# A decoder trunk on one core: parts of GpSimd's S5 preparation on VectorE and ScalarE, the first layer's gated blocks 0 to 7 moved in pairs, tables spread over more units

## The reference, cut to what matters

```
for layer in range(2):
    if layer == 1: kb, vb, kmean = shared_kv(h, kv_norm, w_kv)
    h = h + 0.5 * swiglu(rmsnorm(h, ffn1_norm[layer]), ffn1_w_in[layer], ffn1_w_out[layer])
    hn = rmsnorm(h, mix_norm[layer])
    h = h + (s5_mixer(hn, ...) if layer == 0 else moba_attention(hn, ...))
    h = h + 0.5 * swiglu(rmsnorm(h, ffn2_norm[layer]), ffn2_w_in[layer], ffn2_w_out[layer])
return rmsnorm(h, final_norm)

swiglu(x) = (silu(g) * u) @ w_out,  g, u = split(x @ w_in)
s5_mixer: lambda = exp(a * dt) (complex, 64 states in 64 groups); B' = f(lambda, a) * b
          x[t] = lambda * x[t-1] + B' u[t];  y = Re(C x) + d * u;  gelu(y) @ w_glu, gated
```

## Time and profile before

| | |
|---|---|
| median of 3 runs | 952.15 us (951.94 to 952.48) |
| the profiled execution | 952.85 us |
| its span, first to last instruction | 951.1 us |
| TensorE busy | 938.9 us, 99% |
| VectorE busy | 622.0 us, 65% |
| ScalarE busy | 502.6 us, 53% |
| GpSimd busy | 184.3 us, 19% |
| DMA | 180.11 MB, 189 GB/s |
| granted TensorE clock | 0.999 |

### The profile page before, as it was taken

How to read it: one execution, slowest core, us unless ns; L and a number is a source line. 1 busy time by engine, 2 the same in 40 slices (tenths; PEclk the granted TensorE clock), 3 DMA queues, 4 the chain that set the end, 5 groups by cost and what they waited for, 6 DMA issues and landing times.

```text
span 951.1 us, 14886 instructions
## 1 busy us (share of the span) xinstructions
PE 938.9 (99%) x5809; PEld 777.5 (82%) x5809; DVE 622.0 (65%) x783; ACT 502.6 (53%) x713; POOL 184.3 (19%) x235
## 2 busy tenths in 40 slices
PE   8999999999999999999999999999999999999997
PEld 7888888888888888888888888888888888888885
DVE  5667977889765666655665666666567565666554
ACT  7654544577555455544654454554458554554441
POOL 2799999901000000000000000000060000000000
PEclk9999999999999999999999999999999999999999
DMA  9856555520355777777678677777751367777761
GB/s 333 292 176 201 181 177 194 177 70 4 115 192 189 216 209 215 214 216 221 219 184 253 174 227 213 220 210 235 220 177 46 112 198 218 211 215 205 188 215 45
DMA packets 137877, 180.11 MB, mean 189 GB/s; under 512 B 95184, under 2 KB 95952, under 8 KB 137808
## 3 DMA queue, kind: packets, MB, share of 16 engines
q1 hardware_dynamic: 137232, 178.33, 61.8%
q10 hardware_dynamic: 576, 0.84, 0.3%
HBM read 167.33 MB, written 1.05 MB: 177 GB/s over the span
## 4 chain that ended last, share of the span: by engine, by line
PE 77%; POOL 16%; issue 2%; ACT 1%; DVE 1%; DMA 1%; SPq 1%; POOLq 0%; ACTq 0%; DVEq 0%
PE ps L1417 75%; POOL tmp L592 7%; POOL sm L592 4%; POOL cp L592 2%; POOL w L592 2%; DMA raw<-in_in 1%; PE ps L1446 1%; POOL rotc L592 0%; POOL skip_eye L720 0%; PE ps L1565 0%; POOL rots L592 0%; POOL w_bd L710 0%; PE ps L1422 0%; SPq L530 0%; ACT pr L1014 0%
## 5 line engine op out<-in xcount | busy, mean ns | idle before, releaser
L1064 DVE TENSOR_TENSOR w_lo<-raw,w_hi 128x1024 fp32r<-128x1024 f32 x309 | 397.4, 1291 | 262.1 <-ACT w_hi L779 260.2
L779 ACT ACTIVATE w_hi<-raw 128x1024 fp32r<-128x1024 f32 x309 | 326.4, 1059 | 317.4 <-PE ps L1417 314.9
L1417 PE MATMUL ps<-w_hi,x_hi 128*128 128x512 f32 x896 | 351.1, 392 | 0.6 <-DVE w_lo L1064 0.6
L1417 PE MATMUL ps<-w_hi,x_lo 128*128 128x512 f32 x896 | 348.8, 389 | 0.0
L1417 PE MATMUL ps<-w_lo,x_hi 128*128 128x512 f32 x896 | 348.7, 389 | 0.0
L1417 PEld LDWEIGHTS ps<-w_hi,x_hi 128*128 128x128 f32 x896 | 168.3, 188 | 37.2 <-DVE w_lo L1064 1.4
L1417 PEld LDWEIGHTS ps<-w_hi,x_lo 128*128 128x128 f32 x896 | 168.2, 188 | 35.5
L1417 PEld LDWEIGHTS ps<-w_lo,x_hi 128*128 128x128 f32 x896 | 168.4, 188 | 33.9
L1417 PE MATMUL ps<-w_hi,hid_hi 128*128 128x512 f32 x352 | 137.2, 390 | 0.0
L1417 PE MATMUL ps<-w_hi,hid_lo 128*128 128x512 f32 x352 | 136.9, 389 | 0.0
L1417 PE MATMUL ps<-w_lo,hid_hi 128*128 128x512 f32 x352 | 136.9, 389 | 0.0
(11 more groups left out here) (163 smaller groups left out, 612.5 us busy)
## 6 DMA issues: line engine op xcount, KB each, us to landing
raw<-in_in SPq DMA_DIRECT2D x173, 512.0 KB, 4.5
raw<-in_out SPq DMA_DIRECT2D x88, 512.0 KB, 4.2
raw<-in_glu SPq DMA_DIRECT2D x16, 512.0 KB, 4.4
hid_lo<-prod SPq DMA_DIRECT2D x240, 32.0 KB, 2.7
raw<-in_k SPq DMA_DIRECT2D x8, 512.0 KB, 4.4
raw<-in_v SPq DMA_DIRECT2D x8, 512.0 KB, 4.6
raw<-in_q SPq DMA_DIRECT2D x8, 512.0 KB, 4.3
raw<-in_o SPq DMA_DIRECT2D x8, 512.0 KB, 4.3
```

Source lines behind the costliest of these rows:

```text
L779: act.activation(w_hi[:, gu % WS, :], raw[:, gu % RAW, :], ACT.Copy)\
L1064: dve.tensor_tensor(w_lo[:, gu % WS, :], raw[:, gu % RAW, :], w_hi[:, gu % WS, :].bitcast(F32), ALU.subtract)\
L1417: return pe.matmul(o, w, x, start=start, stop=stop, skip_group_check=True)
```

## The change

- Phase 0's blocks 0 to 7 are handled like the blocks of the later networks (`by_pairs`): VectorE turns them in squares, SyncE moves four pairs into `hid_lo`. Blocks 8 to 10 are still turned by TensorE.
- `skip_eye` is one instruction and is issued before the input's norm.
- The two copies of C into `cp` are ScalarE's (`copy_c`, in unit 14).
- The last power of lambda in `cp` is VectorE's, 6 steps in units 58 to 62 (`C_STEP_AT`, `last_c_step`). Its first step waits for GpSimd's `made["cp"]`; ScalarE's `half_c` waits for its end.
- VectorE's 12 table steps are in units 27 to 42 and 50 to 55.
- GpSimd's `decay_odd` no longer waits for VectorE's tables.
- The mean (L1286, L1406) is folded into the sum of squares, which starts from `end_ms` and scales by 1/D.

```diff
-BATCHES = (0, 4, 8)
+BATCHES = (8,)
-TABLE_AT = (27, 28, 29, 30, 31, 32, 33, 34, 52, 54, 56, 58)
+TABLE_AT = (27, 28, 30, 32, 34, 36, 38, 40, 42, 50, 53, 55)
+C_STEP_AT = (58, 59, 60, 61, 61, 62)
 def pair_number(p, b):
-    return (p.hid0 // p.blocks - 1) * ((p.blocks + 1) // 2) + b // 2
+    if p.n == 0:
+        return b // 2
+    return BATCHES[0] // 2 + (p.hid0 // p.blocks - 1) * ((p.blocks + 1) // 2) + b // 2
+def by_pairs(p, b):
+    return p.name == "in" and (p.n > 0 or b < BATCHES[0])
+def pairs_behind(p, b):
+    return p.n == 0 and b >= 4 and by_pairs(p, b // 2 * 2 - 4)
 def high_behind(p, phases, b, j):
-    if p.n < 2:
+    if p.n < 2 and not pairs_behind(p, b):
         return high_batch(p, phases, b, j)
...
             moves = {p.unit0 + (pair_end(p, b) + 1) * p.upb + MOVE_BEHIND + q: (p, b, q)
-                     for p in phases if p.name == "in" and p.n for b in range(0, p.blocks, 2)
-                     for q in range(QS)}
+                     for p in phases for b in range(0, p.blocks, 2) if by_pairs(p, b) for q in range(QS)}
...
+            pool.wait_ge(par_in, 16)
+            pool.tensor_tensor(skip_eye[:, :, :], eye[:, :].unsqueeze(1).broadcast_to([P, DT, 32]),
+                               skip.unsqueeze(2).broadcast_to([P, DT, 32]), ALU.mult)\
+                .then_inc(skip_ready, 1)
             inverse_rms(None)
...
-            for r in range(2):
-                link(pool.tensor_scalar(cp[:, r, :, 0, :],
-                                        w2[:, r, 0, :, :], 1.0, 0.0, ALU.mult, ALU.add))
+            pool.wait_ge(c_copied, 2)
...
-            for k in range(1, STEP + 1):
+            for k in range(1, STEP):
                 cmul(cp[:, 0, :, k], cp[:, 1, :, k], cp[:, 0, :, k - 1], cp[:, 1, :, k - 1],
                      wide(LR), wide(LI), t(2), t(3))
...
             def half_c(d, g):
                 if d == 0 and g == 0:
                     act.wait_ge(pool_step, made["cp"])
+                    act.wait_ge(c_last, 2)
...
+            def copy_c():
+                act.wait_ge(s5_in, 16 * 2)
+                for r in range(2):
+                    act.activation(cp[:, r, :, 0, :], w2[:, r, 0, :, :], ACT.Copy)\
+                       .then_inc(c_copied, 1)
...
+                        for step, unit in zip(last_c, C_STEP_AT):
+                            if unit == p.unit0 + p.upb * b + j:
+                                step()
...
+            def last_c_step():
+                def wide(i):
+                    return sm[:, i, :].unsqueeze(2).broadcast_to([P, GP, S5_J])
+                def first(k, r, i):
+                    if k == 0 and r == 0 and i == C_RE:
+                        dve.wait_ge(pool_step, made["cp"])
+                        dve.wait_ge(turns_done, 4)
+                    elif k == 0:
+                        dve.wait_ge(c_last, 1)
+                    link(dve.tensor_tensor(tmp[:, k, :].rearrange("p (g j) -> p g j", j=S5_J),
+                                           cp[:, r, :, STEP - 1], wide(i), ALU.mult))
+                def second(r, op):
+                    dve.tensor_tensor(cp[:, r, :, STEP],
+                                      tmp[:, 0, :].rearrange("p (g j) -> p g j", j=S5_J),
+                                      tmp[:, 1, :].rearrange("p (g j) -> p g j", j=S5_J), op)\
+                       .then_inc(c_last, 1)
...
-                link(dve.tensor_tensor_reduce(out=prod[:, :, 0, :], in0=halved(h[:, q, right]),
-                                              in1=halved(h[:, q, right]), scale=1.0, scalar=0.0,
+                dve.tensor_tensor_reduce(out=prod[:, :, 0, :], in0=halved(h[:, q, right]),
+                                              in1=halved(h[:, q, right]), scale=1.0 / D, scalar=end_ms[:, q:q + 1],
                                               op0=ALU.mult, op1=ALU.add,
-                                              accum_out=ss[:, q, 1:2]))
-                dve.scalar_tensor_tensor(end_ms[:, 1, q:q + 1], ss[:, q, 1:2], 1.0 / D,
-                                         end_ms[:, 0, q:q + 1], ALU.mult, ALU.add)\
-                   .then_inc(mix_mean, 1)
+                                              accum_out=ss[:, q, 1:2]).then_inc(mix_mean, 1)
```

More of the change, by code:

```diff
@@ L341, in prod_of @@
         def prod_of(p, b):
-            if p.n == 0:
+            if not by_pairs(p, b):
                 return pair_of(b % BATCH // 2)[:, b % 2]
@@ L701, in _ @@
                      t(2), t(3))
-            for k in range(1, STEP + 1):
+            for k in range(1, STEP):
                 cmul(cp[:, 0, :, k], cp[:, 1, :, k], cp[:, 0, :, k - 1], cp[:, 1, :, k - 1],
                      wide(LR), wide(LI), t(2), t(3))
-            made["cp"] = steps[0]
+            made["cp"], made["lambda"] = steps[0], (LR, LI)
             def mask_w(d):
@@ L717, in make_decay @@
                                    1.0, 0.0, ALU.mult, ALU.add).then_inc(decay_ready, 1)
-            for d in range(DT):
-                pool.tensor_tensor(skip_eye[:, d, :], eye[:, :], skip[:, d:d + 1].broadcast_to([P, 32]),
-                                   ALU.mult).then_inc(skip_ready, 1)
             for d in range(2):
-                if d:
-                    pool.wait_ge(turns_done, 4)
                 pool.memset(decay(d)[:, :, :, 0:1].rearrange("p g r c -> p (g r) c"), 0.0)\
@@ L805, in high_hidden @@
             def high_hidden(p, b):
-                if p.n == 0:
-                    act.wait_ge(hid_turned, min(b // BATCH * BATCH + BATCH, p.blocks))
+                if not by_pairs(p, b):
+                    act.wait_ge(hid_turned, min(b // BATCH * BATCH + BATCH, p.blocks) - BATCHES[0])
                     act.activation(halves(hid_hi[:, 2 * b:2 * b + 2, :].rearrange("p f x -> p (f x)")),
@@ L878, in dense @@
                             s5_angles()
+                        if n == 0 and b == 3 and j == 2:
+                            copy_c()
                         if n == 1 and b == 1 and j >= p.upb - LEAD:
@@ L1258, in half_table @@
                         lambda: second(rots, ALU.add)]
+            def last_c_step():
[14 more added lines that the diff above has]
+                       .then_inc(c_last, 1)
+                C_RE, C_IM = made["lambda"]
+                return [lambda: first(0, 0, C_RE), lambda: first(1, 1, C_IM),
+                        lambda: second(0, ALU.subtract),
+                        lambda: first(0, 0, C_IM), lambda: first(1, 1, C_RE),
+                        lambda: second(1, ALU.add)]
             last_turn = half_table(0) + half_table(1)
+            last_c = last_c_step()
             dve.wait_ge(consts, 2)
```

37 lines of the change are left out of this document (19 added, 18 removed).

## The result

The changed kernel takes **956.46 us** (median of 5 runs, 954.32 to 957.19) against 952.15 us (951.94 to 953.25) for the kernel before on the same chip. The ratio is 1.0032, with a 95% interval of 1.0022 to 1.0043: slower. (The quotient of the two medians is 1.0045, just outside this interval; by either figure the change made the kernel slower.) The prediction was 948.9 us, faster, with a range that ended at 951.2; it was wrong by 7.6 us and in the sign. The profiled execution took 956.46 us, with a span of 954.6 us, 3.5 us more than the span before.

The account below looks back on a forecast made before the run. TensorE, busy 99%, was taken to bound the kernel, with GpSimd's preparation running as long up to S5. The terms -2.7 - 0.65 - 0.2 + 0.3 = -3.25 us took 952.15 to 948.9 us; range 947.8 to 951.2.

Parts of the forecast that it names:

- Step 1: TensorE's turning of blocks 0 to 7 goes, two batches of 1.35 us: minus 2.7 us.
- Step 2: VectorE's transposes and subtractions replace the turning; lateness stays inside a cover of some 5 us: nothing, at most 1 us.
- A: Rival: VectorE stands at unit 58 for GpSimd's cp, conversions queued behind, TensorE waits: 949 to 952, taken as 951 us; chance 0.12.
- B: Rival: as that wait for cp, with transposes contending too, cp at 182.3, TensorE waits 10.2 us: 959.1 us; chance 0.05.
- Step 3: 64 more transfers in SyncE's queue, ScalarE reading pair 0 at about 52 us: nothing, at most 1 us.
- Step 4: GpSimd's list gets shorter: cp at 167.9 instead of 182.4, masks end at 181.5 instead of 190.3; GpSimd leaves the chain.
- Step 5: S5 entry: hn of the second half starts 1.0 us earlier, TensorE gains its idle 0.65 us; bounds nothing or 1.0.
- Step 6: End of the kernel: the small step in the last chain goes, minus 0.2 us (0 to 0.5).
- Step 7: Start: the new skip instruction runs beside VectorE's unit 3 conversion, for which TensorE waits: plus 0.3 us (0 to 0.9).
- C: Rival: turning gained, but the start costs 0.9 us and another wait replaces S5's 0.65: 950.15 us; chance 0.10.
- D: Rival: ScalarE waits for a moved pair or VectorE's fullest block exceeds the cover, 1 to 2 us: about 950.5; chance 0.07.

Follow-up runs that it names:

- after: The changed kernel itself, with all parts of the change, against the kernel before: 956.46 us, ratio 1.0032.
- e2: The changed kernel with the turning of all phase 0 blocks put back on TensorE, all else kept: 951.04 us, ratio 0.9986 to the kernel before.
- e4: The changed kernel with GpSimd's powers of lambda in w2 and cp left out, zeros in their place: 949.49 us, ratio 0.9971 to the kernel before.
- e13: The changed kernel with pairs for blocks 0 to 3 alone, table steps in units 27 to 32, steps on C in units 59 to 62: 949.83 us.
- e3: The kernel before with only blocks 0 to 7 turned by VectorE and moved in pairs, GpSimd's list in full: 956.2 us, ratio 1.0054.
- e8: The kernel before with only the table steps in their new places, units 27 to 42 and 50 to 55: 952.91 us, ratio 1.0016.
- e7: The changed kernel with pairs for blocks 0 to 3 alone and table steps two to a unit in units 27 to 32: 951.55 us, ratio 0.9988.

## Why the prediction was wrong, point by point

**Step 1, the turning: right.** 2.7 us predicted, 1.40 + 1.37 = 2.77 by the ledger of after, and the same in the other kernels with pairs.

**Step 2, what replaces it: the step that failed.** The prediction put VectorE's excess in the units 32 to 35 at 0 to 3 us (13.9 us in 10.9), inside the cover of 5, and the cost to TensorE at nothing, 1 us at most. It measured 2.34 + 3.94 = 6.28 us. Two things were wrong in it.

The first is the size of the stretched operations. All were stretched by the conversions' factor (1.95 for 1.23), which makes 1.1 us of a subtraction or a table step of 0.7. In after the four subtractions took 1.54 to 1.78 and the six table steps 0.76 to 1.77, 1.27 in the mean; the conversions took 2.0 to 2.2 for 1.95. That alone makes 16.2 us of the 13.9 and uses the cover up within the block. The size could have been read in the trace of before, where table steps with two inputs in SBUF stood beside the same 512-column steps of GpSimd, and a subtraction that read PSUM was not stretched:

```profile
104.83 1.79 DVE L1250 TENSOR_TENSOR tmp<-rots,sm 128x512 f32<-128x512 f32 x1
...
108.54 0.68 DVE L1124 TENSOR_TENSOR hid_lo<-ps,hid_hi 128x512 fp32r<-128x512 f32 x1
```

The second is the end of the account: "the next block has no subtraction and no transpose". It has neither, but it has table steps, at 36 and 38 and, behind it, at 40 and 42; the units 41 and 42 have the subtractions of blocks 6 and 7; and with conversions of 2 us nothing of the excess is paid back. The account has to run until the lateness is down to nothing: over the 12 units it is 42 us of VectorE's work against 32.6. The longer window alone would not have sounded the alarm: at the prediction's durations the 12 units are 12 x 1.95 + 10 x 1.1 + 2.4 = 36.8 us, an excess of 4.2, still inside 5. The other 5 us are the sizes.

What showed it is the last of the prediction's own signs of being wrong: a unit of the first layer that takes TensorE longer than 2.72 us, "which no term here foresees".

Of these 6.28 us, 3.08 are waits as the trace counts them. The low clock is a second part: 3.41 us at half speed do 1.7 us of work less. The remainder, some 1.5 us, is at the restarts: from 120.61 to 120.97 one matmul follows another 0.36 us apart instead of 0.227, and a wait shown as 0.25 us moved the position by 0.58. The prediction said that "no term of the sum is one of the clock", which held for the trace of before but not for a change that can make TensorE wait 2 us.

Taking the subtraction from PSUM + SBUF to SBUF + SBUF is what exposed it: with the turning back on TensorE (e2) it takes 0.68 us beside the same GpSimd list. Rivals A and B did let the subtractions stretch, but priced only what GpSimd loses by it (0.9 us each), not what VectorE does.

**Step 3, the transfers: right.** ScalarE reads pair 0 at 52.59 us (predicted 52) and never waits for a transfer:

```profile
52.59 0.62 ACT L824 ACTIVATE hid_hi<-hid_lo 128x512 fp32r<-128x512 f32 x1
```

**Step 4, GpSimd's list: right in its size, and the masks follow TensorE.** Without the pairs (e2_turn_back) cp was ready at 169.3 us, with a start 0.66 us early, for the predicted 167.9 and what contention adds; in after at 171.99. In after the masks were no longer late:

```profile
184.83 3.81 POOL L726 TENSOR_SCALAR w_bd<-w,half 128x512 f32<-128x512 f32 x4 [9.74 <-PE ps L1463]
```

**Step 5, the S5 entry: right in the mechanism, a little small.** The two halves of hn in after and TensorE's turning of them, without an idle before it (0.65 us in the earlier trace rows):

```profile
192.45 0.88 DVE L1340 TENSOR_SCALAR hn<-h,rs 128x512 f32<-128x512 f32 x2 [0.69 <-POOL rs L744]
...
197.81 0.88 DVE L1340 TENSOR_SCALAR hn<-h,rs 128x512 f32<-128x512 f32 x2 [0.68 <-POOL rs L744]
```

```profile
198.40 1.04 PE L1682 MATMUL ps<-ident,hn 128*128 128x128 f32 x8
```

The entry gained 1.04 us by the ledger, in after, e2, e4 and e13, where 0.65 was taken and 1.0 was the upper bound. That mark is VectorE's; TensorE's own gain, from its turning of hn (198.40 against 195.61), is 0.99: the bound, not the 0.65 to which TensorE's other work was to hold it.

**Step 6, the end: right.** From the last residual to the final product VectorE took 2.15 us (948.50 to 950.65) against 2.29 before: 0.14 us for a predicted 0.2.

**Step 7, the start: not decided.** In after the conversion beside the new instruction took 1.50 us and TensorE came 0.27 us later, which is what I had forecast. But the kernels with that instruction stand between -1.00 and +0.27 at the first mark, and those without it (before, e3, e8) between -0.93 and 0. The start varies by more than the term between executions; the match proves nothing.

**The rivals.** A (VectorE stands for cp at unit 58, deciding point 172.1 us) didn't show in after but decided e7: cp at 172.27 us, TensorE 1.43 us later, where the prediction's chain of five conversions gave almost nothing. Three of the five were stretched (1.51, 1.60 and 1.63 for the 1.2 taken) and one step (1.09 for 0.7), so that the last ended 11.7 us after the first step began, not 10.3. B fell: the transposes take 0.712 us beside a full GpSimd, as in the later layers. By the Trainium skill, "GPSIMD Engine Reference", section 1 Specifications, VectorE contends with GpSimd when it has two SBUF inputs; the trace agrees on both sides, for the subtraction (0.72 to 1.54 and more) and for the one-input transpose. C stays undecided with step 7. D had named the right place, "VectorE's fullest block exceeds the cover", with a chance of 0.07 and a price of 1 to 2 us for 6.3. B stood as the only named way to slower than before, and it was made of the wrong one of the two new operations. That the time came out slower, as in B, is no merit of B: GpSimd's cp was ready at 171.99, not 182.3.

## What to carry to other kernels

When work goes to an engine that runs ahead of the bound engine, add up its queue until the lateness is paid back, not for the fullest block: list every operation in the code's order, over all units in which the neighbour engine is busy, each at the duration that a row of its own kind (same operands, same size, same neighbour) shows; the factor of another operation was too small here. A wait of 2 us on TensorE isn't priced at 2 us; look at the granted clock behind it. And where a change has several parts, the mark-by-mark position of the bound engine separates them in one trace, whereas the totals, here between 949.5 and 956.5 us, mix a start that varies by 1 us with everything else.
